# Zeros matmuls at TensorE's waits in a two-block transformer kernel

## The reference

```
h = h + 0.5 * swiglu(rms_norm_2(h, ffn1_norm_g[layer]), ...)      # width 2816
hn = rms_norm_2(h, mix_norm_g[layer])
...  primary = convolution (layer 0) or causal attention of 12 heads (layer 1)
...  mem_out = attention of 4 heads into 256 memory tokens
h = h + concat([primary, mem_out]) @ w_o[layer]
h = h + 0.5 * swiglu(rms_norm_2(h, ffn2_norm_g[layer]), ...)
```

## Time and profile before

| | |
|---|---|
| median of 3 runs | 1939.4 us (1937.99 to 1941.61) |
| profiled execution | 1940.61 us, of which the span is 1938.7 |
| TensorE busy | 1739.1 us (90%), mean granted clock 0.938 |
| VectorE busy | 901.0 us (46%) |
| ScalarE busy | 644.4 us (33%) |
| DMA | 409.96 MB, 211 GB/s over the span |

### The profile page before, as it was taken

One profiled execution on the slowest core, in us unless ns is written; L12 is line 12 of the kernel. 1 busy time (PEld: TensorE's weight loads), 2 busy tenths in 40 slices (PEclk: granted clock), 3 DMA queues, 4 the chain that ended last, 5 costly groups with the idle time before them and its releaser, 6 DMA issues.

```text
span 1938.7 us, 32851 instructions
## 1 busy us (share of the span) xinstructions
PE 1739.1 (90%) x13905; PEld 1466.2 (76%) x13911; DVE 901.0 (46%) x1395; ACT 644.4 (33%) x859; POOL 43.3 (2%) x53
## 2 busy tenths in 40 slices
PE   6997989888888878699999989999899997989998
PEld 6986868545555455499989779998799986469998
DVE  4775455110111101265558755555745557535554
ACT  4544352101111011243334153334343344334332
POOL 2000000000000000000000400000000000000000
PEclk9998988989998999799999989999999998589999
DMA  9543335999999999655654025564355552025560
GB/s 294 184 150 123 109 108 215 417 417 417 418 418 418 417 418 418 242 189 179 194 173 153 1 87 184 184 194 153 115 170 192 184 184 87 22 65 162 184 193 24
DMA packets 191143, 409.96 MB, mean 211 GB/s; under 512 B 6887, under 2 KB 141182, under 8 KB 174700
## 3 DMA queue, kind: packets, MB, share of 16 engines
q1 hardware_dynamic: 189104, 404.55, 57.7%
q0 software_dynamic: 1744, 4.53, 0.9%
q10 hardware_dynamic: 236, 0.06, 0.0%
HBM read 408.06 MB, written 1.05 MB: 211 GB/s over the span
## 4 chain that ended last, share of the span: by engine, by line
PE 74%; DMA 10%; DVE 7%; ACT 4%; SPq 3%; issue 1%; POOL 0%; ACTq 0%; DVEq 0%; POOLq 0%
PE bank L525 18%; PE bank L526 17%; PE bank L527 17%; DMA odd_expert<-in_w_up_dram 9%; PE bank L805 4%; PE bank L848 3%; PE bank L818 3%; SPq L412 3%; DVE wlo L1520 2%; PE bank L979 2%; PE bank L636 2%; PE bank L662 2%; PE bank L837 2%; PE bank L537 1%; ACT whi L1130 1%; DVE prob L1778 1%
## 5 line engine op out<-in xcount | busy, mean ns | idle before, releaser
L1994 DVE TENSOR_TENSOR wlo<-raw,whi 128x2048 fp32r<-128x2048 f32 x120 | 275.1, 2292 | 274.5 <-ACT whi L1405 274.5
L1405 ACT ACTIVATE whi<-raw 128x2048 fp32r<-128x2048 f32 x120 | 229.7, 1914 | 279.1 <-PE bank L527 279.1
L525 PE MATMUL bank<-x1hi,whi 128*128 128x256 f32 x976 | 281.4, 288 | 3.4 <-DVE x1lo L1552 2.0
L526 PE MATMUL bank<-x1hi,wlo 128*128 128x256 f32 x976 | 278.2, 285 | 0.0
L527 PE MATMUL bank<-x1lo,whi 128*128 128x256 f32 x976 | 278.1, 285 | 0.0
L525 PE MATMUL bank<-x0hi,whi 128*128 128x256 f32 x880 | 249.8, 284 | 0.9 <-DVE x0lo L1552 0.9
L526 PE MATMUL bank<-x0hi,wlo 128*128 128x256 f32 x880 | 249.1, 283 | 0.0
L527 PE MATMUL bank<-x0lo,whi 128*128 128x256 f32 x880 | 249.0, 283 | 0.0
L1520 DVE TENSOR_TENSOR wlo<-raw,whi 128x2048 fp32r<-128x2048 f32 x71 | 162.1, 2289 | 95.2 <-ACT whi L1130 94.9
L525 PEld LDWEIGHTS bank<-x1hi,whi 128*128 128x128 f32 x976 | 189.5, 194 | 7.6 <-issue 6.4
L526 PEld LDWEIGHTS bank<-x1hi,wlo 128*128 128x128 f32 x976 | 189.5, 194 | 1.6 <-issue 0.7
(11 more groups left out here) (290 smaller groups left out, 2471.4 us busy)
## 6 DMA issues: line engine op xcount, KB each, us to landing
raw<-in_ffn_w_gate_dram SPq DMA_DIRECT2D x44, 1024.0 KB, 5.3
raw<-in_ffn_w_up_dram SPq DMA_DIRECT2D x44, 1024.0 KB, 5.3
raw<-in_ffn_w_down_dram SPq DMA_DIRECT2D x44, 1024.0 KB, 5.0
raw<-in_w_gate_dram SPq DMA_DIRECT2D x32, 1024.0 KB, 17.9
raw<-in_w_up_dram SPq DMA_DIRECT2D x32, 1024.0 KB, 21.3
raw<-in_w_down_dram SPq DMA_DIRECT2D x32, 1024.0 KB, 21.0
odd_expert<-in_w_gate_dram SPq DMA_DIRECT2D x32, 1024.0 KB, 22.3
odd_expert<-in_w_up_dram SPq DMA_DIRECT2D x32, 1024.0 KB, 22.7
```

Of the source, the lines that this page charges most:

```text
L525: pe.matmul(dst, a_hi, b_hi, start=first, stop=False, skip_group_check=True)
L526: pe.matmul(dst, a_lo, b_hi, start=False, stop=False, skip_group_check=True)
L1405: act.activation(whi[:, c0_ % SPLIT, :], raw[:, c0_ % RAW, :], ACT.Copy).then_inc(hi_ready, 1)
L1994: dve.tensor_tensor(wlo[:, c0_ % SPLIT, :], raw[:, c0_ % RAW, :], whi[:, c0_ % SPLIT, :].bitcast(F32), ALU.subtract).then_inc(lo_ready, 1)
```

## The change

A helper `keep_busy(times, bank)` issues `times` matmuls of the zeros tile, 128 rows by 128 columns of weights and 512 moving columns, into a bank that nobody reads until something else has written it with `start=True`. It has no semaphore of its own. 226 such matmuls are added:

- ahead of the turn at seven stage boundaries: 14 before the cross attention's queries, 48 after the experts, 16 after each of SwiGLU 0, 1 and 2, 14 before SwiGLU 1 and 14 before SwiGLU 3,
- 6 between the turn and the router's products,
- 54 around the last mixer's query norms, in the bank of its first projection, whose reader has finished (a wait on `evac_v` stands ahead of them),
- 2 in each of steps 2 to 15 of the last mixer's heads, between the scores and the turns.

TensorE also waits for `zero_ready` at its very start. No other engine's list changes.

```
+            def keep_busy(times, bank):
+
+                for _ in range(times):
+                    pe.matmul(bank[:, :], zeros[:, 0:P], zeros[:, :], start=True, stop=True, skip_group_check=True)
+
@@ -675,6 +680,7 @@
+            pe.wait_ge(zero_ready, 1)
             pe.wait_ge(in_c, 16)
@@ -748,6 +754,7 @@
+            keep_busy(14, ps[4])
             turn(xn, (xn_ready, 6))
@@ -776,6 +783,7 @@
             turn(xn, (xn_ready, 10))
+            keep_busy(6, ps[4])
             x_ready()
@@ -1025,8 +1033,10 @@
+            keep_busy(48, ps[4])
             turn(xn, (xn_ready, 12))
             swiglu(0, 1)
+            keep_busy(16, ps[7])
             turn(xn, (xn_ready, 14))
@@ -1062,9 +1072,11 @@
+            keep_busy(14, ps[5])
             turn(xn, (xn_ready, 16))
             swiglu(1, 0)
 
+            keep_busy(16, ps[7])
             turn(xn, (xn_ready, 18))
@@ -1094,18 +1107,27 @@
             linear_cols(c0 + 3, 1)
+            spare = linear_bank(c0)
             rotate(qb_t[:, 0:2, :], hs + 2)
+            pe.wait_ge(evac_v, evac_count[c0][1])
+            keep_busy(8, spare)
             head_sums()
+            keep_busy(14, spare)
 
             def beside_heads(step):
 
                 if step == 0:
                     rotate(qb_t[:, 2:4, :], hs + 3)
+                    keep_busy(8, spare)
                     head_sums()
+                    keep_busy(16, spare)
                 if step == 1:
                     rotate(qb_t[:, 4:6, :], hs + 4)
+                    keep_busy(8, spare)
                 if step == 2:
                     pe.wait_ge(rope_done, 6)
+                if 2 <= step < 16:
+                    keep_busy(2, spare)
```

## The result

| | before | after |
|---|---|---|
| median of the runs, us | 1940.51 (1937.99 to 1942.69, 4 runs) | 1905.42 (1901.49 to 1906.22, 4 runs) |
| profiled execution, us | 1940.61 | 1901.49 |
| its span; mean granted clock | 1938.7; 0.938 | 1899.5; 0.973 |

The ratio is 0.982, 95% interval 0.9803 to 0.9836: 35 us faster, where 26 were forecast. The direction and the main term came out, the sum was 9 us short.

The account below looks back on a forecast made before the run. TensorE at half clock was taken to bound the last mixer's heads. Heads 17.0, norms 0 and boundaries 9.2 sum to 26.2 us off 1940.6, forecast 1914; range 1906 to 1925 for 8 in 10.

Parts of the forecast that it names:

- the main term: Last mixer's heads run at granted clock 1.00 instead of 0.50 nearly throughout; heads together gain 17.0 us.
- a to c: Last mixer's heads: causal steps gain 11.1 us, steps 12 to 16 gain 7.3, entry loses 1.4; together 17.0.
- (c): Entry to the last mixer's heads: one short low stretch of some 3.3 us allowed; loses 1.4 us.
- (a): Heads' nine causal steps 3 to 11: 2.65 us instead of 3.88, set by VectorE and ScalarE; gains 11.1 us.
- (d): Last mixer's query norms with 54 zeros: gains up to 2 us, losses up to 3; taken as 0.
- Its reason: Heads' scores use 64 of the array's 128 rows, keeping the clock low; zeros use all 128 and raise it.
- The in-step zeros as the means: Two zeros matmuls per head step bring the higher clock and cost almost nothing beside VectorE and ScalarE's loop.
- (e): Zeros at stage boundaries, behind the experts and before the router fill idle time and hold the clock; gains 9.2 us.
- 6 zeros hold the clock a little longer, of 17 low us: 0.9: Before the router: six zeros keep the higher clock slightly longer in a 17 us low stretch; gains 0.9 us.
- the one behind the experts: Behind the experts: 48 zeros, about 12 us, lie beside a wait of 12.52 us; gains 0.8 us.
- Other stalls move onto new low stretches: Rival of no effect: all later work shifts and stalls elsewhere bring new low stretches; 1940 us, chance 2%.

Follow-up runs that it names:

- e11: Changed kernel with 62 instead of 48 zeros behind the experts and a burst of 12 before step 2's wait replacing the heads' 28: 1898.9 us, ratio 0.9788.
- e9: Kernel before plus only the last mixer's norm zeros and one burst of 12 ahead of step 2's wait, none in head steps: 1920.3 us, ratio 0.9904.
- e6: Kernel before plus only the heads' 28 zeros, each over 64 rows instead of 128: 1925.2 us, ratio 0.9928.
- e13: Kernel before, no zeros, every score in the last mixer's heads computed twice: 1958.5 us, ratio 1.0095.
- e7: Kernel before plus only the last mixer's norm zeros and heads' zeros in steps 2 to 5: 1923.0 us, ratio 0.9921.
- e3: Kernel before plus only the 54 zeros around the last mixer's query norms, none in head steps or at boundaries: 1940.4 us, ratio 1.0008.
- e2: Kernel before plus only the boundaries' and router's zeros, none in the last mixer: 1920.5 us, ratio 0.9895.
- e5: Kernel before plus only the six zeros ahead of the router: 1932.1 us, ratio 0.9966.
- e15: Kernel before plus only six zeros 85 us earlier, ahead of the cross-attention's turns, none at the router: 1938.75 us, ratio 0.9996.
- e1: Kernel before plus only the last mixer's zeros, around its norms and in its head steps: 1924.6 us, ratio 0.9919.
- e8: Changed kernel with 62 zeros behind the experts instead of 48: 1906.1 us.
- e4: Kernel before plus only the 28 zeros in the last mixer's head steps: 1926.6 us, ratio 0.9928.
- e14: Kernel before plus only one bf16 zeros matmul in each of head steps 2 to 15: 1925.4 us, ratio 0.992.

## Why the prediction was right in kind and short in size

- **The clock in the heads (a to c).** Right in mechanism: 1.00 for nearly all of them, entered at 0.50 for one short stretch, as (c) had it. The norms and heads gave 17.0 us, the forecast for (a) to (d), but that it is the same number is in part luck. A causal step at 1.00 is 2.50 to 2.62 us against 2.65 taken, about 1 us more gained over nine; the low stretch at the entry is 6.8 us against 3.3 taken, and costs about 1 us more; 1 us came at the norms' side. The loop of VectorE and ScalarE was not the bound at 2.65: without zeros a step is 2.45 (e11), with them TensorE sets it.
- **Its reason.** Not borne out as given. Idle rows of the scores do not hold the clock down by themselves: the same heads run at 1.00 without any zeros once they are entered so (e9). Whether the zeros' 128 rows are what raised it is open, since zeros over 64 rows did as well but shared steps with scores on the other 64 (e6). The inference rested on one rise, with the scores gone; the part that survives is that more scores don't raise the clock (e13) and other matmuls do.
- **The in-step zeros as the means.** Half right. They bring the clock up, but nothing needs them once it is up (e7, e9).
- **The norms (d).** Right: 0 alone (e3). In the changed kernel 0.9 us of the 17.0 lie there.
- **The boundaries (e).** The miss lies here: 19 us alone (e2) for 9.2. The step that failed is the router's: "6 zeros hold the clock a little longer, of 17 low us: 0.9". I counted the zeros' own reach into the router and not what follows. 3 us of the router's 0.21 us matmuls at twice the rate are some 3 us less already, the low stretch ends sooner, and the one behind it, at 302, doesn't come. Found: 5.0 in the profiled execution and 4.0 in e5's, and 6.6 by medians between two kernels with six zeros each (e5, e15), of which their profiled executions place 3.9 at the router. The other terms of (e) came within 0.7 us, but for the one behind the experts.
- **What was not in the sum.** The sum had only places with zeros. Stalls without any kept the clock too: the kernel before is at 0.50 from 1114 to 1121, 1131 to 1135, 1363 to 1367 and 1397 to 1401 us, and the changed one at 1.00 in the same work, which gave 1.2 us at the convolution's wait and 2.5 at the key norms. All five profiled executions with zeros at the boundaries show this, and those of e1 and e15, with no zeros near, show 1.2 and 0.8 of it, so it hangs on where a stall falls; no run isolates it. With the 3.3 at the experts' end and 2.1 in the first 40 us, where kernels without zeros lie anywhere between 1.4 lost and 3.7 gained, they are 9 us of the profiled difference. "Other stalls move onto new low stretches" was a rival for the bad side alone; it went to the good side.
- **Behind the experts.** 0 for 0.8. Filling the wait gives 1.00 and 0.2 to 0.4 us (e8, e11), since VectorE sets the pace.
- **The median.** The profiled execution was the fastest of its four runs, 3.9 us below their median. By medians 9 us were missed; by the profiled ones 13.

"TensorE: Matmul & The Clock Gate" in the Trainium skill, section "Why this matters for your kernels", asks for continuous activity of TensorE. The trace disagrees: 55.2 of 55.2 us busy stood at 0.50. The opposite case, 31.0 of 34.0 us busy at 1.00 (e9), does not speak against it, since that section allows short gaps and the longest wait in these heads is 0.8 us.

## What to carry to other kernels

Look in a trace for stretches that are at the lower clock although TensorE is never idle: there, a few zeros matmuls of another kind than the work itself, or better a burst that fills the wait ahead of the stretch, can change its level to the end (here 13 us of 1940 with zeros in the steps alone, e4, and 18 with those of the norms and the burst, e9). Place zeros in waits that end in TensorE's own work; where another engine sets the pace behind the wait, the higher clock gives nothing (e8). And when such a change is priced, the low stretch is to be followed through all that comes behind it until another engine or a transfer takes over, and a single stretch's gain is no upper bound.

## What the runs showed of the hardware

- The same stream of matmuls has two lasting states, 0.50 with TensorE busy for 55.2 of 55.2 us (kernel before) and 1.00 with 31.0 of 34.0 (e9), and a wait ahead of it of 2.4 us, open (e3) or filled (e9), chose between them. In e1's profiled execution that wait was only 0.70 us, and the heads were entered at 1.00 unfilled.
- More work of TensorE does not by itself end the low state: one bf16 zeros matmul of 0.43 us a step ended it (e14), 1.28 us of further scores a step didn't (e13).
- Two matmuls on different halves of the rows ran at the same time: zeros on rows 0 to 63 started 0.01 us behind scores on rows 64 to 127, and the step was no longer for them (3.88 us at 0.50, e6).
- The clock can fall without a gap in TensorE's records: in the changed kernel the router's matmuls (36 columns each, 0.11 us apart) run at 1.00 from 275.54 and at 0.50 from 278.7 (3.06 of 3.06 us busy in the window above).
- An idle of 2.7 us named "issue" behind the experts' loop was gone when six zeros matmuls were added far ahead of it (e15); the median didn't move.
